# Pairing the high and low part of a half-filled tile in the expert layer of a two-layer backbone

## The reference, cut to what matters

```python
def moe_swiglu(h, router_w, w_gu, w_down):        # h: (B, L, 1024); 8 experts of inner width 1408
    probs = jax.nn.softmax((h @ router_w).astype(jnp.float32), axis=-1)
    top_p, top_i = lax.top_k(probs, TOP_K)        # TOP_K = 2
    top_p = top_p / jnp.sum(top_p, axis=-1, keepdims=True)
    gates = jnp.sum(jax.nn.one_hot(top_i, N_EXPERTS) * top_p[..., None], axis=-2)
    y = jnp.zeros_like(h)
    for e in range(N_EXPERTS):                    # swiglu: (silu(gate) * up) @ w_down
        y = y + gates[..., e:e + 1] * swiglu(h, w_gu[e], w_down[e])
    return y
```

## Time and profile before

| | us |
|---|---|
| median of 3 runs | 2005.14 |
| the profiled execution | 2005.26 |
| its span, first to last instruction | 2003.7 |
| the eight experts, 1260.41 to 1953.6 | 693.2 |
| two-tile experts 1 and 2 | 94.88 and 93.82 |
| three-tile expert 7 | 143.00 |

### The profile page before, as it was taken

One profiled execution on the slowest core, in us unless ns is written; L12 is line 12 of the kernel. 1 busy time (PEld: TensorE's weight loads), 2 busy tenths in 40 slices (PEclk: granted clock), 3 DMA queues, 4 the chain that ended last, 5 costly groups with the idle time before them and its releaser, 6 DMA issues. The chain is left out here.

```text
span 2003.7 us, 39774 instructions
## 1 busy us (share of the span) xinstructions
PE 1909.0 (95%) x14669; PEld 1552.6 (77%) x14670; DVE 1121.5 (56%) x1761; ACT 752.6 (38%) x1296; POOL 431.6 (22%) x360
## 2 busy tenths in 40 slices
PE   7899999999999999999999998999999999999995
PEld 5788888888876478887888776788887787787872
DVE  4676777677674644224122367665558558554337
ACT  4542442343241122221223102654547457453332
POOL 0345334435422222121121243100000000000003
PEclk9899999999999999999999999999999999999997
DMA  8234234224325353253222624976569669664344
GB/s 285 89 120 139 70 101 146 95 90 134 110 81 192 106 163 106 77 150 117 87 88 89 213 74 152 339 260 212 189 215 333 209 208 331 239 211 148 111 148 173
DMA packets 184793, 320.53 MB, mean 160 GB/s; under 512 B 26113, under 2 KB 77209, under 8 KB 184555
## 3 DMA queue, kind: packets, MB, share of 16 engines
q1 hardware_dynamic: 170283, 286.00, 43.1%
q0 software_dynamic: 8144, 28.84, 3.9%
q10 hardware_dynamic: 6128, 2.30, 0.4%
HBM read 284.41 MB, written 32.67 MB: 158 GB/s over the span
## 5 line engine op out<-in xcount | busy, mean ns | idle before, releaser
L1381 PE MATMUL pp<-whi,xTh 128*128 128x512 f32 (+1 forms) x1152 | 442.5, 384 | 15.0 <-issue 6.8
L1382 PE MATMUL pp<-whi,xTl 128*128 128x512 f32 (+1 forms) x1152 | 431.6, 375 | 2.1 <-issue 2.1
L1383 PE MATMUL pp<-wlo,xTh 128*128 128x512 f32 (+1 forms) x1152 | 431.7, 375 | 0.0
L2121 ACT ACTIVATE whi<-raw_halves 128x1024 fp32r<-128x1024 f32 (+1 forms) x256 | 245.3, 977 | 112.5 <-PE pp L1383 98.1
L1381 PEld LDWEIGHTS pp<-whi,xTh 128*128 128x128 f32 x1152 | 218.5, 190 | 55.1 <-issue 10.4
L1383 PEld LDWEIGHTS pp<-wlo,xTh 128*128 128x128 f32 x1152 | 218.4, 190 | 41.4 <-issue 2.8
L1382 PEld LDWEIGHTS pp<-whi,xTl 128*128 128x128 f32 x1152 | 218.7, 190 | 35.3
L2770 DVE TENSOR_TENSOR wlo<-raw_halves,whi 128x1024 fp32r<-128x1024 f32 (+1 forms) x144 | 167.5, 1163 | 109.4 <-ACT whi L2121 82.7
L1381 PE MATMUL pp<-whi,hTh 128*128 128x512 f32 x503 | 202.3, 402 | 4.4 <-DVE ybuf L2722 2.3
L2779 DVE TENSOR_TENSOR wlo<-raw_halves,whi 128x1024 fp32r<-128x1024 f32 (+1 forms) x144 | 159.2, 1105 | 78.5 <-ACT whi L2121 64.5
L1383 PE MATMUL pp<-wlo,hTh 128*128 128x512 f32 x503 | 196.7, 391 | 0.4 <-issue 0.4
(11 more groups left out here) (355 smaller groups left out, 3291.2 us busy)
## 6 DMA issues: line engine op xcount, KB each, us to landing
raw_halves<-in_moe_w_gu SPq DMA_DIRECT2D x320, 256.0 KB, 4.3
wring<-in_ada_w SPq DMA_DIRECT2D x80, 512.0 KB, 4.7
raw_halves<-in_moe_w_down SPq DMA_DIRECT2D x160, 256.0 KB, 3.4
wring<-in_ffn_w_gu SPq DMA_DIRECT2D x80, 256.0 KB, 2.9
wring<-in_dn_w_in SPq DMA_DIRECT2D x124, 128.0 KB, 2.9
wring<-in_ffn_w_down SPq DMA_DIRECT2D x40, 256.0 KB, 3.0
expert_in<-zeros SPq DMA_DIRECT2D x36, 256.0 KB, 3.3
wring<-in_ada_first SPq DMA_DIRECT2D x32, 256.0 KB, 5.7
```

What stands on the lines that cost most here:

```text
L1381: pe.matmul(out, hi[:, c0 + c, tt], wh, start=(first and c == 0), stop=False)
L1382: pe.matmul(out, lo[:, c0 + c, tt], wh, start=False, stop=False)
L1383: mm = pe.matmul(out, hi[:, c0 + c, tt], wl, start=False, stop=(last and c == nk - 1))
L2121: act.activation(whi[:, hs, 0:nk, 0:w], raw_half(l, k, s)[:, 0:nk, 0:w], ACT.Copy)\
```

## The change

A tile with at most 64 rows leaves half of PE's 128 columns of a weight load unused. For experts of two or three tiles that end so, the rows are shifted by 64: the first tile is the half one, with its rows in 64 to 127. ACT copies, for every chunk, the 64 columns of the low part and the 64 of the high part side by side into one block of 128 (`PAIR`; `pair_copy`). The half tile then takes two matmuls per chunk, that block by high and by low weights (`halved`, L1435 and L1436 of the changed kernel), instead of three. The sums of the low rows land in PSUM rows 0 to 63 and have to be added to rows 64 to 127: ACT copies them out (`low_copy`) and a matmul with a shifted identity adds them (`fold_low`), 8 times per expert, 7 of 512 columns and one of 256. The fold stands behind the other tiles of the last half for the first five gate and up groups and for the last down group, and behind the second tile of the next half for the other two. SiLU of all tiles of a paired expert waits for the fold. PE's loop body now holds each expert twice, in `pe.If(paired > 0)` and `pe.Else()`. ACT gets a branch on the same flag. The other edits: 3 more DVE steps in the chain that works out the counts, 14 zero transfers in a row behind the dense layer's weights and 4 more among them, one more table value read per expert, and experts of over 384 rows run five tiles.

```diff
-                def nest(n, body, t=0):
+                def nest(n, body, paired, t=0):
                     body(t)
-                    if t + 1 < T:
-                        if isinstance(n, int):
-                            nest(n, body, t + 1)
+                    if t + 1 < (3 if paired else T):
+                        if isinstance(n, int) or t == OVER_ALL or paired and t == 0:
+                            nest(n, body, paired, t + 1)
                         else:
                             with pe.If(n > t + 1):
-                                nest(n, body, t + 1)
+                                nest(n, body, paired, t + 1)
...
+                        def halved():
+                            if m == 0:
+                                pe.wait_ge(S["pair_ready"], earlier * 7 + 1)
+                            elif 24 <= m < 30:
+                                pe.wait_ge(S["pair_ready"], earlier * 7 + 2 + (m - 24))
+                            for c in range(nk):
+                                wh, wl = whi[:, hs, c, 0:width], wlo[:, hs, c, 0:width]
+                                pair = hi[:, c0 + c, PAIR]
+                                pe.matmul(out, pair, wh, start=(first and c == 0), stop=False)
+                                mm = pe.matmul(out, pair, wl, start=False, stop=(last and c == nk - 1))
+                            mm.then_inc(S["low_ps"] if last else f["half_done"], 1)
...
+                def fold_low(i, earlier, b, width, done):
+                    pe.wait_ge(S["low_sb"], earlier * 8 + (i + 1))
+                    pe.matmul(bank(b)[:, 0:width], fold[:, :], low_sums[:, 0:width], start=False, stop=True,
+                              skip_group_check=True).then_inc(done, 1)
...
                         for i in range(2):
                             n, c = this_expert(pe, rn, rc)
-                            n2 = expert(2 * pair + i, n, c)
-                            next_expert(pe, rn, rc, n, n2)
+                            paired, earlier = this_half(pe, rh, rs)
+                            with pe.If(paired > 0):
+                                n2, h2 = expert(2 * pair + i, n, c, earlier)
+                                next_expert(pe, rn, rc, n, n2)
+                                next_expert(pe, rh, rs, 1, h2)
+                            with pe.Else():
+                                n2, h2 = expert(2 * pair + i, n, c)
+                                next_expert(pe, rn, rc, n, n2)
+                                pe.reg_mov(rh, h2)
...
+                        elif t == 0:
+                            with act.If(single[0] > 0):
+                                low_copy(j, 5 * (j % 2), 2 * w, single)
+                                act.wait_ge(f["gu_ps"], q0 + n)
+                                act.activation(hbuf[:, 0, 0:w], bank(5 * (j % 2))[:, 0:w], ACT.Silu).then_inc(f["sil_done"], 1)
+                            with act.Else():
+                                one()
...
+                def low_copy(i, b, w, single):
+                    act.wait_ge(S["low_ps"], single[1] * 8 + (i + 1))
+                    act.activation(low_sums[0:HB, 0:w], bank(b)[0:HB, 0:w], ACT.Copy).then_inc(S["low_sb"], 1)
+                def pair_copy(buf, k0, nk, single, signal, count):
+                    with act.If(single > 0):
+                        act.wait_ge(f[signal], count)
+                        act.activation(buf[:, k0:k0 + nk, 1, PAIR].rearrange("p k (s t) -> p k s t", s=2),
+                                       buf[:, k0:k0 + nk, :, HB:P], ACT.Copy).then_inc(S["pair_ready"], 1)
```

More of the change, by code:

```diff
@@ L41 @@
 LEVELS = 7
-SLOTS = 18
+SLOTS = 21
+OVER_ALL = 3
+PAIR = slice(4 * 128, 5 * 128)
 HALVES = 4
@@ L158, in xs_groups @@
     if i < len(groups):
-        with eng.If(n2 > groups[i][0]):
-            xs_groups(eng, m, n2, body, groups[i][0], i)
+        with eng.If(n2 > min(groups[i][0], OVER_ALL)):
+            xs_groups(eng, m, n2, body, T - 1 if groups[i][0] >= OVER_ALL else groups[i][0], i)
 def half_rows(k, s):
@@ L713, in _ @@
                         row_load(g2_rows[r].rearrange("p a n -> p (a n)"), mod_dram[0, r, 5 * D:6 * D], "g2_in")
+            for part in range(36, ZERO_IN):
+                zero_in(part)
+            for part in range(36, ZERO_OUT):
+                zero_out(part)
             ring.base += 36
@@ L1376, in tile @@
                             ahead(t)
-                        tt = slice(t * P, (t + 1) * P)
-                        for c in range(nk):
-                            wh, wl = whi[:, hs, c, 0:width], wlo[:, hs, c, 0:width]
-                            out = bank(bk(t))[:, 0:width]
-                            pe.matmul(out, hi[:, c0 + c, tt], wh, start=(first and c == 0), stop=False)
-                            pe.matmul(out, lo[:, c0 + c, tt], wh, start=False, stop=False)
-                            mm = pe.matmul(out, hi[:, c0 + c, tt], wl, start=False, stop=(last and c == nk - 1))
@@ L1384, in tile, with whole @@
-                        mm.then_inc(done if last else f["half_done"], 1)
+                        out = bank(bk(t))[:, 0:width]
+                        def whole():
+                            tt = slice(t * P, (t + 1) * P)
+                            for c in range(nk):
+                                wh, wl = whi[:, hs, c, 0:width], wlo[:, hs, c, 0:width]
+                                pe.matmul(out, hi[:, c0 + c, tt], wh, start=(first and c == 0), stop=False)
+                                pe.matmul(out, lo[:, c0 + c, tt], wh, start=False, stop=False)
+                                mm = pe.matmul(out, hi[:, c0 + c, tt], wl, start=False, stop=(last and c == nk - 1))
+                            mm.then_inc(done if last else f["half_done"], 1)
@@ L1416, in ffn @@
                         mm.then_inc(f["xsT_ps"], 1)
-                    for t in range(1, T):
+                    for t in range(1, OVER_ALL + 1):
                         with pe.If(n0 > t):
@@ L1452, in expert @@
                             half(e, 4 * j + s, n, xTh, xTl, 2 * s, bk, s == 0, s == 3, f["gu_ps"],
-                                 512 if j < 5 else 256, free, after, ahead)
+                                 512 if j < 5 else 256, free, after, ahead, earlier)
+                            if earlier is not None and s == 3 and j < 5:
+                                fold_low(j, earlier, bk(0), 512, f["gu_ps"])
                             if l and j == 1 and s == 0:
                                 n2 = next_count(pe, e)
+                                h2 = next_half(pe, e)
                     if l:
@@ L2257, in first_high @@
                     .then_inc(S["slot_hi"], 1)
+            act.wait_ge(S["pool_const"], 4)
+            act.activation(fold[:, HB:P], ident[:, 0:HB], ACT.Copy)
             first_high(0, 0)
```

190 lines of the change are left out of this document (128 added, 62 removed).

## The result

The changed kernel took 2026.55 us (median of 4 runs, 2025.64 to 2034.13), the kernel before 2005.69 beside it (4 runs, 2002.26 to 2010.3): a ratio of 1.011, 95% interval 1.0092 to 1.0129. It is 21 us slower where 18 us faster was forecast, and lies where the second rival, "jumps decide, slower", put it (2029).

What follows compares the result with a forecast made beforehand. PE, busy 95% of the span, was taken as the bound: 39.9 us saved less 22.2 of costs, 15.7 of them jumps, gave 17.7 us, so 1987 us from about 2005. The range was 1971 to 2007.

Steps and rivals of the forecast that it cites:

- jumps decide, slower: Rival: every jump in PE's expert loop is exposed, seven at 8.2 us with the lower clock, giving 2029 us; chance 0.14.
- 4 to 5 and 6 to 7: one jump behind two tiles, covered: 0: Between these experts PE's sequencer is far enough ahead after two-tile work to hide one jump: 0 us.
- into expert 0 ... cover it: Ahead of expert 0, 80 matmuls of selection stand before the jump and hide it: 0 us.
- the lead taken off at 2 to 3: Between experts 2 and 3, two jumps cost 9.4 us less a sequencer lead of 5 to 7, leaving 3.5.
- 0 to 1: Jump over paired code behind a one-tile expert: 2.9 us of gap and 2.3 of lower clock, 5.2.
- 2 to 3, 3 to 4: Two jumps in each place: 5.8 us with lower clock at the first, 4.7 more behind the old jump back.
- rival "covered": Rival: the new jumps cost nothing, through code fetched far ahead or a longer lead, giving 1972 us; chance 0.17.
- The gain of the matmuls: In experts 2, 6 and 7 PE saves 13.3 us each, net of the folds' own matmuls: 39.9 us.
- 39.9 less 2.4, 0.5, 0.6 and 0.5: Pairing's gain less fold waits at experts' ends, in whole halves, the later tail, and expert 7's third-tile bank.
- ACT as the bound: Rival: in paired experts ACT's weight copies start late at each of 24 folds, 23 us, giving 2007; chance 0.13.
- Side edits: Edits beside the pairing, such as the counts' chain (0.5 us) and ACT's branches with the table read (2.0).
- the 2.0 us for them: In the three one-tile experts, ACT's added branches and the second table read, PE waiting partly for transfers: 2.0 us.

Runs made afterwards that it cites:

- e3: Changed kernel with no expert paired and PE's paired code dropped, so only the side edits remain and no long jumps: 2012.05 us, ratio 1.004.
- e1: Changed kernel with PE's two long codes made one, short tests inside for the paired tile and folds, same matmuls: 1996.24 us, ratio 0.9969.
- e2: Changed kernel with its table made to pair no expert, both long codes kept, so each expert jumps over the paired one: 2060.85 us, ratio 1.0295.
- e7: e3 with 90 matmuls (180 instructions) that never run, jumped over at the head of each expert: 2025.32 us, ratio 1.0097.
- e4: Changed kernel with some of PE's long jumps announced, those ahead of experts 1, 3, 5 and 7: 2016.06 us, ratio 1.0072.
- e5: e1 with no expert paired, so the short tests stay but nothing is paired: 2024.64 us, ratio 1.0089.
- e9: e3 with seven matmuls that never run added behind the fifth tile's code in each half, no test or jump added: 2024.25 us, ratio 1.0095.
- e10: e3 with code for three tiles instead of five in each routed expert: 1993.35 us, ratio 0.9939.
- e11: e1 with code for three tiles instead of five in each routed expert: 1979.75 us, ratio 0.9876.
- e6: e1 with each half first testing for more than one tile, the first tile's code standing there once more: 2024.95 us, ratio 1.009.

## Why the prediction was wrong

**The step that failed is "4 to 5 and 6 to 7: one jump behind two tiles, covered: 0", with "into expert 0 ... cover it" and the lead taken off at 2 to 3.** It rested on a reading of the earlier trace rows: code fetched 5 us before PE got there was taken as the sequencer's lead. That jump back is announced. What the row showed was the announcement (or the announcement and a lead; they can't be told apart there), and none of the new jumps had one. The comparison with e3 (unpaired experts and the start) and with e1 (paired ones), window by window, gives the jumps' cost, clock included:

| jump | forecast | measured | from |
|---|---|---|---|
| into 0 | 0 | 3.2 | from the count's matmul to expert 0: 20.2 against 17.0 |
| 0 to 1 | 5.2 | 6.2 | windows 0 and 1: 3.5 + 2.7 |
| 2 to 3, 3 to 4 | 5.8 + 4.7 | 16.6 | windows 2 and 3: 11.2 + 5.4 |
| 4 to 5 | 0 | 5.6 | windows 4 and 5: 2.7 + 2.9 |
| 6 to 7 | 0 | 7.0 | windows 6 and 7: 4.3 + 2.7 |
| sum | 15.7 | 38.6 | |

That is 23 of the 40 us between forecast and result, 16 of them in three jumps priced at zero, 6 in the two places with two jumps (16.6 against 10.5) and 1 behind expert 0. Seven jumps at 5.5 us each are above the 4.8 at which the rival said the gain turns into a loss. I had given this rival 0.14. It was right in mechanism, but that its 2029 came within 3 us of the result is luck: its 57.4 us for the jumps were 19 too many, and what the pairing, the side edits and the part without a cause lost beyond the forecast filled that up. The rival "covered" is out: a jump over 1449 instructions, which it counted as fetched already, cost 6.1 us in e2. e2 and e7 rule out a fixed price of the jump itself, and e4 points to the fetch in it.

The Trainium skill, "Runtime: NRT & Kernel Launch", section "Instruction fetch mechanics", says that a taken branch out of the prefetched window forces a fetch before execution goes on. The trace agrees: three blocks came within the 10.15 us ahead of expert 3. I had quoted it and then let a lead that it doesn't mention cover three jumps.

**The gain of the matmuls** was right in kind: L1435 and L1436 stand 210 times each, PE's busy time is 39.1 us less in e1 than in e5 (1877.7 against 1916.8) where 39.9 was forecast, and expert 6 saved 11.7 us net, of 13.3 forecast less its fold's wait. Experts 2 and 7 saved 8.2 and 8.4. In all the pairing gave 28.4 us by the medians, where the forecast's terms (39.9 less 2.4, 0.5, 0.6 and 0.5) make 35.9. The largest waits that go with it stand in the changed kernel's timeline:

```profile
1435.36 0.50 PE L1450 MATMUL pp<-low_sums,fold 128*128 128x512 f32 x1 [1.89 <-ACT low_sums L2276]
1950.56 0.50 PE L1421 MATMUL pp<-whi,hT 128*128 128x512 f32 x1 [1.79 <-ACT ybuf L2292]
```

The first is a fold in expert 2's first group, the second the third tile's bank in expert 7, free only when ACT has copied all three tiles behind the fold, and both are followed by steps at half clock. In e1 they are 1.16 us, without the lower clock, and 1.80, with seven steps at it (1.4 us more): 4.4 us together. The forecast had 0.5 for all folds in whole halves and 0.5 for the third tile's bank (for SiLU, not for the copies), so they make about half of the missing 7.5. No kernel here takes these two waits away, so this is read, not shown, and the other half is open. The folds as a whole cost little, 2.4 us of idle, and 22 of the 24 near none. That the forecast had 2.4 too is luck: it had put 1.0, 1.0 and 0.4 at the ends of the experts and nearly nothing elsewhere, and measured are 1.89 in a whole half of expert 2 and 0.49 at its end.

**ACT as the bound** fell: ACT is busy 54 and 55 us of expert 2 and 6, and PE's idle time before folds is 2.4 us in all where that rival had 23. **Side edits** were 7 us against 2.5. And that one-tile experts wait for transfers, as I took from the earlier trace rows and on which the 2.0 us for them rested, was a misreading: a DMA share of 0.97 does not say what PE waits for. e9 and e10 show that the code's length held these experts up already before: with 3.7 blocks less they are 5.5 us shorter, with the transfers at 1.00.

The three parts (23 for the jumps, 7.5 for the pairing, 4.5 for the side edits) make 35 of the 39.6 us. The rest has no cause shown; it is no more than the start of the dense layer differs by from trace to trace. In the profiled execution some of it lies behind expert 7: that stretch is 3.8 us longer than before (53.8 against 50.0) where 1.2 was forecast, the last fold with its wait and the later stores. In the other kernels that pair it is 51.5 to 52.9 us, in those that pair nobody 50.0 to 50.4 and in two of them 51.1 (e7) and 51.6 (e5), so what is above the 1.2 stays open.

## What to carry to other kernels

Code that doesn't run isn't free: price a second version of a long body by its jumps (here 6 us each without an announcement, and 17 us for two places where two followed each other) before the matmuls it saves. Code inside the body that short work has to step over costs as well: here about 1.5 us for each block more up to 12 blocks, and nearer 5 beyond. Where short items step over code for long ones, cut the code first: here leaving out two unused tiles gave 19 us (e10 against e3), about what the change cost. A fetch that came in good time behind an announced jump says nothing safe about a jump that isn't announced.

## What the runs showed of the hardware

- The length of PE's code held up the one-tile experts though most of it was only stepped over: 50.6 us with 6.2 blocks of some 16 KB (0.10 MB in 6 packets), 56.1 with 9.9, 59.4 with 11.9 and 68.4 with 13.8, while the transfers moved 281 to 356 GB/s. The profile shows it only as small waits of "issue".
- A forward jump on PE over 1449 instructions cost 6.1 us on average (e2 against e3), one over 180 instructions 1.7 (e7). Behind one-tile experts a jump back followed at once by a jump over 1449 instructions left 9.1 to 10.2 us (the changed kernel and e2), behind two-tile expert 1 it left 2.9 (e2).
- Announcing an unconditional jump at the head of the code before it took 2.5 to 3.2 us off a gap of 5.9 to 10.2 (e4, two places); of two announced conditional jumps one gained nothing (5.08 to 4.98 us). The announced jump back left 3.4 and 4.0 us behind one-tile experts with 2543 instructions an expert (e3), 3.5 and 4.5 with 2055 (e11), and nothing with 1596 (e10); but 0.4 ahead of expert 4 with 3531 (e6), so length alone doesn't decide it.
- PE's steps were at the 1.2 GHz level behind a gap of as little as 1.8 us (1950.56 above), and at 2.4 GHz behind one of 2.77 (1740.83): the length of the gap alone doesn't decide it.
